# Attention queries rotated without their 1/rms, which scales the softmax exponential instead

## The chip, the core and the metric

The kernel runs on one core of one Trainium2 chip. The metric is the device time of one execution in microseconds (us); lower is better. A core has five engines with a queue of instructions each: TensorE (PE in the profile; its weight loads are listed as PEld), VectorE (DVE), ScalarE (ACT), GpSimd (POOL) and SyncE (SP), which issues most of the DMAs. They meet only at semaphores.

## What is computed

Two layers of a block with feed-forward, a mixer of windowed attention and gated linear attention, and a second feed-forward, for 256 tokens and 256 context tokens of width 1024. The change concerns the attention queries alone:

```python
q = axial_rope(rmsnorm(aq.reshape(B, S, ATTN_HEADS, ATTN_HEAD_DIM), q_norm_w), tabs)
k = axial_rope(rmsnorm(ak.reshape(B, S, ATTN_KV_HEADS, ATTN_HEAD_DIM), k_norm_w), tabs)
...
s_win = jnp.einsum('bnqhgd,bnkhd->bnhgqk', qb, kw).astype(jnp.float32) * scale
...
p = jax.nn.softmax(jnp.concatenate([s_win, s_ctx, s_sink], axis=-1), axis=-1).astype(v.dtype)
```

There are 8 query heads and 2 key heads of 128 dimensions. `rmsnorm` divides each query (one token of one head) by the root of its mean square and multiplies each dimension by a weight. `axial_rope` rotates pairs of dimensions by an angle of the token, for the 256 tokens of x only. In the first layer the context has queries too (512 in all), in the second only the 256 tokens of x.

## The kernel before

**Tiling.** Activations lie turned, with the feature on the 128 partitions and the tokens along the row: hH and hL hold the normed input as a high part in fp32r and the rest. Weights come in units of 1024 x 256 in `raw`; ScalarE casts each unit to WH (`prep`, line 683, two instructions), VectorE subtracts it to get WL (`prep`, line 1118, two), and TensorE makes three products for each pair of tiles (`unit_cols`, lines 1826, 1827 and 1832; `tile_cols`, lines 1846, 1847 and 1851), 24 for an output tile and 48 for a unit. Two unit buffers alternate. Sums land in PSUM, in the eight banks of PS.

**The stage that is changed** is `attn_proj`. Unit n is the values, n+1 the keys, n+2 to n+5 the queries (two heads each). In its loops j = 1 is the keys and j = 2 to 5 the query units; each has two tiles, one for a head, of 512 tokens (first layer; the keys in both) or 256. A tile goes through these steps, each on one engine:

- `squares` (ACT, line 814): PSUM to qsq.
- `qk_sums` (PE, line 2195): a plain fp32 product of qsq with a matrix of ones, which sums over the partitions and leaves the sum in every one of them, in bank 6 or 7.
- `rsq` (ACT, lines 821 and 824): logarithm and exponential, which gives 1/rms in qrs.
- `normed` (DVE, line 1425): PSUM times the weight times qrs, into qn.
- `swaps` (PE, line 2200): a plain fp32 product that exchanges the dimensions of each pair; it overwrites the PSUM bank of the unit.
- `cosines`, `sines`, `rotated` (DVE, lines 1433, 1438 and 1443): the two products and their sum.
- `split` (ACT, line 830) and `low` (DVE, line 1450): the high and the low part for the score products.

**What sets the order.** Every engine's order is written out by hand; nothing is scheduled. PE does a unit, then `swaps` of two units back and `qk_sums` of the unit before, and then the next unit. After n+5 come the first gate tile, `swaps(4)`, `qk_sums(5)`, the scores of the first set, the second gate tile with `swaps(5)` in its middle, and the third.

**Attention** follows, in sets of one key head and 128 queries: 8 in the first layer and 4 in the second. For a set PE makes `scores` (lines 1812 to 1814), DVE takes the maximum and forms the negative bias in two small steps (`maxima`, lines 1484 to 1492), ACT takes the exponential with the constant factor SCALE (`exps`, line 865), DVE divides (`scale`, line 1509), PE turns the probabilities in blocks (`turns`, line 2234; ACT and DVE split them, lines 876 and 1519) and multiplies them with the values. Gate tiles stand between. Line 2004 is used elsewhere: a product with `fold`, which adds the four quarters of 32 partitions. Line 1223 is a reduction of VectorE that first turns each block of 32 x 32. Line 1983 is a product with 32 columns of weights, four of which fill the four quarters of the output partitions.

Of the kernel before, what the change touches and what calls it, by code (L numbers as in the profile page):

```python
# [13 lines left out]
P = 128  # L14
D = 1024
LN_EXP = "natural_log_exp_and_others"
KT = D // P
# [86 lines left out]
def hybrid_backbone(nc, a, out):  # L104

    ctx = ExitStack()
    with ctx:
# [30 lines left out]
        epsc = sb("epsc", [P, 2])  # L138
# [5 lines left out]
        rstd = sb("rstd", [P, T2])  # L144

# [57 lines left out]
        cond_in = sem("cond_in")  # L203
# [4 lines left out]
        sink_in = sem("sink_in")  # L208
# [62 lines left out]
        qk_rot = sem("qk_rot")  # L271
        qk_hi = sem("qk_hi")
# [90 lines left out]
        def keys(qb):  # L363

            return (0, NTB) if qb < 2 else (S, 2)

# [110 lines left out]
        def _(sp):  # L477
# [50 lines left out]
            sp.dma_start(negsink[:], a["attn_sink"].rearrange("l h -> (l h)").partition_broadcast(P)).then_inc(sink_in, 16)  # L528
# [78 lines left out]
        def _(pool):  # L607
            nc.gpsimd.memset(epsc[:, 0:1], EPS)
            nc.gpsimd.memset(epsc[:, 1:2], 1.0).then_inc(eps_ready, 1)
# [50 lines left out]
        def _(act):  # L660
            act.dma_start(ident[:], a["c_ident"]).then_inc(ident_in, 16)
            act.dma_start(rows[0:16, 2, :], a["cond_rows"]).then_inc(cond_in, 16)
# [139 lines left out]
            def attn_proj(l):  # L802
                n = START[("attn_proj", l)]

                act.wait_ge(half_done, 2 * (n + 1))
                for b in (0, 2):
                    nc.scalar.copy(vH[:, b:b + 2, :], PS[:, 2 * b:2 * b + 2, 0:UW]).then_inc(v_hi, 1)

                def squares(j):
                    act.wait_ge(half_done, 2 * (n + j + 1))  # L810
                    for e, (t, T) in enumerate(qk_tiles(l, j)):
                        if t >= 2:
                            act.wait_ge(qk_ss, t - 1)
                        nc.scalar.activation(qsq[:, e, 0:T], PS[:, 2 * (j % 3) + e, 0:T], ACT.Square).then_inc(qk_sq, 1)

                def rsq(j):
                    for e, (t, T) in enumerate(qk_tiles(l, j)):
                        act.wait_ge(qk_ss, t + 1)
                        if t >= 2:
                            act.wait_ge(qk_n, t - 1)  # L820
                        nc.scalar.activation(qrs[:, e, 0:T], PS[:, 6 + e, 0:T], ACT.Ln, bias=epsc[:, 0:1], scale=1.0 / P).then_inc(qk_ln, 1)
                    for e, (t, T) in enumerate(qk_tiles(l, j)):
                        act.wait_ge(qk_ln, t + 1)
                        nc.scalar.activation(qrs[:, e, 0:T], qrs[:, e, 0:T], ACT.Exp, scale=-0.5).then_inc(qk_rs, 1)

                def split(j):
                    for e, (t, T) in enumerate(qk_tiles(l, j)):
                        act.wait_ge(qk_rot, t + 1)
                        dst = kH[:, e, 0:T] if j == 1 else actH[:, 2 * (j - 2) + e, 0:T]
                        nc.scalar.copy(dst, qn[:, e, 0:T]).then_inc(qk_hi, 1)  # L830

                for j in range(1, 6):
                    prep(n + j + 1)
                    squares(j)
                    if j > 1:
                        rsq(j - 1)
                    if j > 2:
                        split(j - 2)
                prep(n + 7)
                gate_copy(l, 0, 0)  # L840
                rsq(5)
                split(4)
                exps(l, 0)
                gate_copy(l, 1, 7)
                split(5)
                gate_copy(l, 2, 6)

# [263 lines left out]
        def _(dve):  # L1111
# [300 lines left out]
            def attn_proj(l):  # L1412
# [6 lines left out]
                def normed(j):  # L1419
                    for e, (t, T) in enumerate(qk_tiles(l, j)):  # L1420
                        dve.wait_ge(qk_rs, t + 1)
                        if t >= 2:
                            dve.wait_ge(qk_ready, t - 1)
                        w = vecT[:, K_NORM + l:K_NORM + l + 1] if j == 1 else vecT[:, Q_NORM + l:Q_NORM + l + 1]
                        nc.vector.scalar_tensor_tensor(qn[:, e, 0:T], PS[:, 2 * (j % 3) + e, 0:T], w, qrs[:, e, 0:T],
                                                       ALU.mult, ALU.mult).then_inc(qk_n, 1)

                def cosines(j):
                    for e, (t, T) in enumerate(qk_tiles(l, j)):
                        dve.wait_ge(qk_n, t + 1)  # L1430
                        if t >= 2:
                            dve.wait_ge(qk_rot, t - 1)
                        nc.vector.tensor_tensor(qt[:, e, 0, :], qn[:, e, 0:S], ropeC[:], ALU.mult)
# [6 lines left out]
                def rotated(j):  # L1440
                    for e, (t, T) in enumerate(qk_tiles(l, j)):
                        dve.wait_ge(qk_parts, t + 1)
                        nc.vector.tensor_tensor(qn[:, e, 0:S], qt[:, e, 0, :], qt[:, e, 1, :], ALU.add).then_inc(qk_rot, 1)

                def low(j):
                    for e, (t, T) in enumerate(qk_tiles(l, j)):
# [3 lines left out]
                        nc.vector.tensor_tensor(lo, qn[:, e, 0:T], hi.bitcast(F32), ALU.subtract).then_inc(qk_ready, 1)  # L1450

                for j in range(1, 6):
                    prep(n + j + 1)
                    if j > 2:
                        cosines(j - 2)
                        sines(j - 2)
                        rotated(j - 2)
                        low(j - 2)
                    if j > 1:
                        normed(j - 1)  # L1460
                cosines(4)
                sines(4)
                rotated(4)
                prep(n + 7, only=0)
                low(4)
                normed(5)
                maxima(l, 0)
                cosines(5)
                sines(5)
                scale(l, 0)  # L1470
                rotated(5)
                low(5)
                prep(n + 7, only=1)

            def maxima(l, i):

                A0, (kv, qb) = set0[l], SETS[l][i]
                k0, nkb = keys(qb)
                for e in range(2):
# [10 lines left out]
                    nc.vector.scalar_tensor_tensor(small[:, 8 + 2 * e:10 + 2 * e], small[:, two], -SCALE, ns, ALU.mult, ALU.min).then_inc(at_negmax, 1)  # L1490
                    dve.wait_ge(at_negmax, done + 1)
# [283 lines left out]
            for l in range(DEPTH):  # L1775
                if l:
                    norm(3 * l)
                if l == 0:
                    dve.wait_ge(sink_in, 16)
# [27 lines left out]
        def _(pe):  # L1807
# [210 lines left out]
            pe.wait_ge(ident_in, 16)  # L2018
            pe.wait_ge(cond_in, 16)
# [164 lines left out]
            def attn_proj(l):  # L2184
                n = START[("attn_proj", l)]
                if l == 0:
                    pe.wait_ge(const_in, 16 * 4)
                first_two(3 * l + 1, rows_high, rows_low, 2, 1)

                def qk_sums(j):  # L2190
                    for e, (t, T) in enumerate(qk_tiles(l, j)):
                        pe.wait_ge(qk_sq, t + 1)
                        if t >= 2:
                            pe.wait_ge(qk_ln, t - 1)
                        mm(PS[:, 6 + e, 0:T], ones[:], qsq[:, e, 0:T], start=True, stop=True).then_inc(qk_ss, 1)

                def swaps(j):
                    for e, (t, T) in enumerate(qk_tiles(l, j)):
                        pe.wait_ge(qk_n, t + 1)
                        mm(PS[:, 2 * (j % 3) + e, 0:S], swap[:], qn[:, e, 0:S], start=True, stop=True).then_inc(qk_swap, 1)  # L2200

                for j in range(2, 6):
                    if j == 2:
                        pe.wait_ge(v_ready, 2 * l + 2)
                    elif j > 3:
                        pe.wait_ge(qk_parts, tile0 * l + 2 * (j - 3))
                    unit_cols(n + j, 2 * (j % 3), hH, hL, qtokens(l))
                    if j > 2:
# [4 lines left out]
                swaps(4)  # L2213
                qk_sums(5)
                scores(l, 0)
                pe.wait_ge(qk_ln, tile0 * (l + 1))
                gate_cols(l, 1, 7, 0, KT // 2)
                swaps(5)
                gate_cols(l, 1, 7, KT // 2, KT)
# [334 lines left out]
```

## Time and profile before

| | us |
|---|---|
| median of 3 runs | 2237.07 |
| lowest and highest | 2236.84, 2237.15 |
| the profiled execution | 2237.79 |
| its span, first to last instruction | 2235.9 |
| TensorE busy | 2211.9 |
| VectorE busy | 1391.4 |
| ScalarE busy | 901.9 |

The granted TensorE clock is 1.0 of full speed in the run's record. The span is read as a chain: at each moment some engine does what the end depends on. A time in the tables is the length of an instruction as recorded; matmuls overlap in the pipeline, so the distance between two starts, not the length, is what one costs its engine.

### The profile page before, as it was taken

What the parts mean: (1) busy time and instruction counts of PE and PEld (TensorE: products, weight loads), DVE (VectorE), ACT (ScalarE), POOL (GpSimd) and SP (SyncE); (2) the same over time, 40 slices, a digit from 0 to 9 for tenths busy, and PEclk for the clock granted to TensorE, in tenths of its full rate; (3) what the DMA queues carried; (4) which work ended last, traced back from release to release, by engine and by line L of the source; (5) the groups of instructions that cost most, each with busy time, mean ns of one, the idle gap of its engine ahead of it and who ended that gap; (6) DMA issues with size and microseconds to landing.
All of it is one profiled execution on the core that took longest, in us unless ns stands there. A gap on an engine that the chain in (4) does not pass through costs nothing.

```text
span 2235.9 us, 29911 instructions
## 1 busy us (share of the span) xinstructions
PE 2211.9 (99%) x12353; PEld 1926.3 (86%) x12353; DVE 1391.4 (62%) x1919; ACT 901.9 (40%) x1352; POOL 194.5 (9%) x264
## 2 busy tenths in 40 slices
PE   8999999999999999999999999999999999999999
PEld 7888888878888888888888898888889899999997
DVE  6988822568566564586763267665236967676754
ACT  4223212456644453342322143222126666555442
POOL 0000000000333340000000000000000033330000
PEclk9999999999999999999999999999999999999999
DMA  9776523210322212346552236565323233336864
GB/s 318 218 230 187 180 97 101 87 50 29 95 76 64 88 58 94 113 138 197 157 168 94 95 113 199 179 187 169 113 95 96 60 114 114 114 116 195 245 180 160
DMA packets 300383, 300.84 MB, mean 135 GB/s; under 512 B 9648, under 2 KB 267288, under 8 KB 300248
## 3 DMA queue, kind: packets, MB, share of 16 engines
q1 hardware_dynamic: 299648, 298.69, 43.2%
q8 instruction: 98, 1.61, 0.3%
q14 instruction: 37, 0.30, 0.0%
q10 hardware_dynamic: 600, 0.25, 0.0%
HBM read 297.86 MB, written 1.05 MB: 134 GB/s over the span
## 4 chain that ended last, share of the span: by engine, by line
PE 90%; DVE 5%; POOL 2%; ACT 1%; issue 1%; DMA 1%; SPq 0%; DVEq 0%; ACTq 0%
PE PS L1826 14%; PE PS L1827 14%; PE PS L1832 14%; PE PS L1813 6%; PE PS L1814 6%; PE PS L1812 6%; PE PS L1846 4%; PE PS L1851 4%; PE PS L1847 4%; PE PS L2361 2%; PE PS L2420 1%; PE PS L2372 1%; DVE WL L1118 1%; PE PS L2097 1%; PE PS L2096 1%; PE PS L2095 1%
## 5 line engine op out<-in xcount | busy, mean ns | idle before, releaser
L1118 DVE TENSOR_TENSOR WL<-raw,WH 128x1024 fp32r<-128x1024 f32 x412 | 497.6, 1245 | 344.4 <-ACT WH L683 343.5
L683 ACT CAST WH<-raw 128x1024 fp32r<-128x1024 f32 x412 | 412.5, 1048 | 376.9 <-PE PS L1814 259.5
L1826 PE MATMUL PS<-hH,WH 128*128 128x512 f32 (+1 forms) x1536 | 542.2, 363 | 1.3 <-DVE sg L1383 0.9
L1827 PE MATMUL PS<-hL,WH 128*128 128x512 f32 (+1 forms) x1536 | 538.5, 361 | 0.0
L1832 PE MATMUL PS<-hH,WL 128*128 128x512 f32 (+1 forms) x1536 | 335.4, 361 | 0.0
L1826 PEld LDWEIGHTS PS<-hH,WH 128*128 128x128 f32 x1536 | 290.1, 189 | 46.4 <-issue 1.2
L1827 PEld LDWEIGHTS PS<-hL,WH 128*128 128x128 f32 x1536 | 290.5, 189 | 43.9 <-issue 1.2
L1832 PEld LDWEIGHTS PS<-hH,WL 128*128 128x128 f32 x1536 | 264.0, 189 | 44.1
L1146 DVE SCALAR_TENSOR_TENSOR mraw<-mraw,cst 128x1024 f32<-128x1024 f32 x196 | 242.5, 1280 | 18.3 <-DMA mraw<-in_w_mod 17.3
L1812 PE MATMUL PS<-hidH,WH 128*128 128x512 f32 (+1 forms) x576 | 214.6, 373 | 0.0
L1813 PE MATMUL PS<-hidL,WH 128*128 128x512 f32 (+1 forms) x576 | 214.1, 372 | 0.0
L1814 PE MATMUL PS<-hidH,WL 128*128 128x512 f32 (+1 forms) x576 | 214.1, 372 | 0.0
L791 ACT ACTIVATE sg<-PS 128x512 f32<-128x512 f32 (+1 forms) x44 | 24.0, 545 | 288.1 <-PE PS L1832 279.6
L1846 PE MATMUL PS<-hH,WH 128*128 128x512 f32 (+1 forms) x384 | 128.9, 348 | 0.0
L1812 PEld LDWEIGHTS PS<-hidH,WH 128*128 128x128 f32 x576 | 108.6, 188 | 19.0
L1813 PEld LDWEIGHTS PS<-hidL,WH 128*128 128x128 f32 x576 | 108.6, 188 | 18.9
L1814 PEld LDWEIGHTS PS<-hidH,WL 128*128 128x128 f32 x576 | 108.6, 188 | 18.5
L1847 PE MATMUL PS<-hL,WH 128*128 128x512 f32 (+1 forms) x384 | 124.4, 336 | 0.0
L785 ACT ACTIVATE sg<-PS 128x512 f32<-128x512 f32 (+1 forms) x44 | 24.0, 545 | 211.0 <-PE PS L1832 206.3
L1387 DVE TENSOR_TENSOR sg<-sg,PS 128x512 f32<-128x512 f32 (+1 forms) x44 | 27.3, 620 | 126.4 <-ACT sg L791 126.3
L1851 PE MATMUL PS<-hH,WL 128*128 128x512 f32 (+1 forms) x384 | 93.4, 337 | 0.0
L1641 DVE TENSOR_TENSOR dq<-dq,gkq 128x1024 f32<-128x1024 f32 (+1 forms) x56 | 62.1, 1110 | 47.3 <-ACT dq L986 46.9
(261 smaller groups left out, 3511.8 us busy)
## 6 DMA issues: line engine op xcount, KB each, us to landing
raw<-in_ffn_w SPq DMA_DIRECT2D x176, 512.0 KB, 5.2
mraw<-in_w_mod SPq DMA_DIRECT2D x132, 512.0 KB, 4.7
raw<-in_w_in SPq DMA_DIRECT2D x52, 1024.0 KB, 5.3
raw<-in_ffn_w SPq DMA_DIRECT2D x44, 1024.0 KB, 4.9
raw<-in_w_branch_attn SPq DMA_DIRECT2D x8, 1024.0 KB, 5.2
raw<-in_w_branch_gla SPq DMA_DIRECT2D x8, 1024.0 KB, 5.1
raw<-in_w_out SPq DMA_DIRECT2D x8, 1024.0 KB, 5.1
mfirst_b<-in_w_mod SPq DMA_DIRECT2D x8, 512.0 KB, 11.9
```

The lines of the kernel that those rows point to most:

```text
L683: nc.scalar.copy(half(WH, n % 2, e, rows), half(raw, n % 2, e, rows)).then_inc(hi_ready, 1)
L1118: nc.vector.tensor_tensor(half(WL, n % 2, e, rows), half(raw, n % 2, e, rows), half(WH, n % 2, e, rows).bitcast(F32), ALU.subtract).then_i ...
L1146: ins = nc.vector.scalar_tensor_tensor(mod_sums(c), mod_buf(p), by, mod_sums(c), ALU.mult, ALU.add)
L1812: mm(o, wh, ah, start=start, stop=False, skip_group_check=rest)
L1813: mm(o, wh, al, start=False, stop=False, skip_group_check=rest)
L1814: return mm(o, wl, ah, start=False, stop=stop, skip_group_check=rest)
L1826: mm(o, wh[:, kt, cols], rh[:, kt, 0:T], start=kt == 0, stop=False)
L1827: mm(o, wh[:, kt, cols], rl[:, kt, 0:T], start=False, stop=False)
L1832: ins = mm(o, wl[:, kt, cols], rh[:, kt, 0:T], start=False, stop=kt == KT - 1)
L1846: mm(o, wh[:, kt, cols], rh[:, kt, 0:T], start=kt == 0, stop=False)
L1847: mm(o, wh[:, kt, cols], rl[:, kt, 0:T], start=False, stop=False)
L1851: ins = mm(o, wl[:, kt, cols], rh[:, kt, 0:T], start=False, stop=kt == KT - 1)
```

## The change

**Queries are rotated without 1/rms.** The rotation is linear, so the factor can be applied later: a score of a query is the unscaled score times the query's 1/rms times SCALE. That factor differs by query, and in the scores a query is a partition, so it is a per-partition factor of the exponential. ScalarE copies the query tile out of PSUM times the weight (`weighted`), into qn or qrs by turns, and `rsq` and `normed` remain for the keys alone (`k_rsq`, `k_normed`).

**The squares are summed another way.** VectorE reduces the squares in turned blocks of 32 x 32 (`square_sums`, one instruction for both tiles), so that a token's four partial sums lie in four quarters of the partitions; TensorE adds the quarters with `fold`, for four heads at a time, in four products of 32 output partitions and 16 or 8 columns (`q_sums`). ScalarE takes the root of 16 or 8 columns (`q_rsq`) into rq. The matrix of ones is used for the keys alone.

**The bias** of the exponential needs one more small step on VectorE in `maxima`, since it must be multiplied by a factor of the query.

**Order and buffers.** `swaps(1)` stands between the two tiles of unit n+3, and `swaps(j)` behind unit n+j. Two buffers are new (640 bytes per partition together); all that is laid out behind them moves up by 640 bytes. Two semaphores are merged into others: `cond_in` into `ident_in` and `sink_in` into `const_in`.

New names:

```diff
+        qred = sb("qred", [P, HEADS * T2 // 32])
+        rq = sb("rq", [P, HEADS * NTB])
...
+        def rotated_buf(j):
+
+            return qn if j % 2 else qrs
+
+        def squares_buf(l, j):
+
+            return qsq[:].rearrange("p e t -> p (e t)")[:, 0:2 * (T2 if j == 1 else qtokens(l))]
```

ScalarE:

```diff
+                    if j == 2:
+                        act.wait_ge(qk_ss, 2 * (l + 1))
+                    elif j > 2:
+                        act.wait_ge(q_red, 4 * l + j - 2)
...
+                def weighted(j):
+                    act.wait_ge(half_done, 2 * (n + j + 1))
+                    if j == 2:
+                        act.wait_ge(qk_n, 2 * (l + 1))
+                    else:
+                        act.wait_ge(qk_ready, tile0 * l + 2 * (j - 2))
                     for e, (t, T) in enumerate(qk_tiles(l, j)):
...
+                        nc.scalar.activation(rotated_buf(j)[:, e, 0:T], PS[:, 2 * (j % 3) + e, 0:T], ACT.Copy,
+                                             scale=vecT[:, Q_NORM + l:Q_NORM + l + 1]).then_inc(q_n, 1)
+
+                def q_rsq(g):
+                    own = slice(g * GRP * qtokens(l) // P, (g + 1) * GRP * qtokens(l) // P)
+                    act.wait_ge(q_tot, 2 * l + g + 1)
+                    nc.scalar.activation(rq[:, own], PS[:, 6, own], ACT.Ln, bias=epsc[:, 2:3]).then_inc(q_ln, 1)
+                    act.wait_ge(q_ln, 2 * l + g + 1)
+                    nc.scalar.activation(rq[:, own], rq[:, own], ACT.Exp, scale=-0.5).then_inc(q_rs, 1)
...
-                for j in range(1, 6):
-                    prep(n + j + 1)
...
+                prep(n + 2)
+                squares(1)
+                prep(n + 3)
+                squares(2)
+                k_rsq()
+                weighted(2)
+                prep(n + 4)
+                split(1)
+                for j in range(3, 6):
+                    if j > 3:
+                        prep(n + j + 1)
+                    if j == 5:
+                        q_rsq(0)
+                    weighted(j)
                     squares(j)
...
+                    split(j - 1)
                 prep(n + 7)
                 gate_copy(l, 0, 0)
...
-                                             scale=SCALE, accum_out=small[:, 16 + g:17 + g])
+                                             scale=head_scales(l)[:, GRP * kv + g, qb:qb + 1], accum_out=small[:, 16 + g:17 + g])
```

VectorE:

```diff
+                def square_sums(j):
+                    dve.wait_ge(q_sq, 8 * l + 2 * (j - 1))
+                    own = slice((j - 2) * qtokens(l) // 16, (j - 1) * qtokens(l) // 16)
+                    nc.vector.tensor_reduce(qred[:, own], squares_buf(l, j).rearrange("p (b i) -> p b i", i=32), AX.X, ALU.add,
+                                            apply_transpose=True).then_inc(q_red, 1)
...
+                dve.wait_ge(q_rs, 2 * l + kv + 1)
...
-                    nc.vector.scalar_tensor_tensor(small[:, 8 + 2 * e:10 + 2 * e], small[:, two], -SCALE, ns, ALU.mult, ALU.min).then_inc(at_negmax, 1)
-                    dve.wait_ge(at_negmax, done + 1)
+                    by = head_scales(l)[:, GRP * kv + 2 * e:GRP * kv + 2 * e + 2, qb]
+                    nc.vector.scalar_tensor_tensor(small[:, 8 + 2 * e:10 + 2 * e], small[:, two], -1.0, by, ALU.mult, ALU.mult).then_inc(at_negmax, 1)
+                    dve.wait_ge(at_negmax, 2 * done + 1)
+                    nc.vector.tensor_tensor(small[:, 8 + 2 * e:10 + 2 * e], small[:, 8 + 2 * e:10 + 2 * e], ns, ALU.min).then_inc(at_negmax, 1)
+                    dve.wait_ge(at_negmax, 2 * done + 2)
```

TensorE:

```diff
+                def q_sums(g):
+                    pe.wait_ge(q_red, 4 * l + 2 * (g + 1))
+                    pe.wait_ge(qk_ln, 2 * (l + 1))
+                    w = GRP * qtokens(l) // P
+                    parts = qred[:, 4 * g * w:4 * (g + 1) * w].rearrange("p (x u) -> p u x", u=4)
+                    for u in range(4):
+                        lanes = slice(32 * u, 32 * u + 32)
+                        ins = mm(PS[lanes, 6, g * w:(g + 1) * w], fold[:, lanes], parts[:, u], start=True, stop=True)
+                    ins.then_inc(q_tot, 1)
...
-                for j in range(2, 6):
...
-                    unit_cols(n + j, 2 * (j % 3), hH, hL, qtokens(l))
-                    if j > 2:
-                        swaps(j - 2)
-                    qk_sums(j - 1)
...
+                pe.wait_ge(v_ready, 2 * l + 2)
+                unit_cols(n + 2, 4, hH, hL, qtokens(l))
+                k_sums()
+                unit_cols(n + 3, 0, hH, hL, qtokens(l), between=3 * [nothing] + [lambda: swaps(1)] + 3 * [nothing])
+                swaps(2)
+                pe.wait_ge(qk_parts, tile0 * l + 2)
+                unit_cols(n + 4, 2, hH, hL, qtokens(l))
+                swaps(3)
+                q_sums(0)
+                pe.wait_ge(qk_parts, tile0 * l + 4)
+                unit_cols(n + 5, 4, hH, hL, qtokens(l))
+                swaps(4)
                 pe.wait_ge(qk_parts, tile0 * l + 6)
                 gate_cols(l, 0, 0)
...
+                swaps(5)
+                q_sums(1)
                 scores(l, 0)
...
+                gate_cols(l, 1, 7)
+                pe.wait_ge(q_ln, 2 * (l + 1))
                 gate_cols(l, 2, 6)
```

**ScalarE in the first layer**, from the cast of unit n+2 on, before (qsq are squares, qrs<-PS the logarithm, qrs<-qrs the exponential, WH a cast):

```order
L683 CAST WH<-raw 128x8x128 x2
L814 ACTIVATE qsq<-PS 128x512 x2
L683 CAST WH<-raw 128x8x128 x2
L814 ACTIVATE qsq<-PS 128x512 x2
L821 ACTIVATE qrs<-PS,epsc 128x512 x2
L824 ACTIVATE qrs<-qrs 128x512 x2
L683 CAST WH<-raw 128x8x128 x2
L814 ACTIVATE qsq<-PS 128x512 x2
L821 ACTIVATE qrs<-PS,epsc 128x512 x2
L824 ACTIVATE qrs<-qrs 128x512 x2
```

and changed (line 853 is `weighted`, 867 `split`):

```order
L702 CAST WH<-raw 128x8x128 x2
L835 ACTIVATE qsq<-PS 128x512 x2
L702 CAST WH<-raw 128x8x128 x2
L835 ACTIVATE qsq<-PS 128x512 x2
L841 ACTIVATE qrs<-PS,epsc 128x512 x2
L844 ACTIVATE qrs<-qrs 128x512 x2
L853 ACTIVATE qrs<-PS,vecT 128x512 x2
L702 CAST WH<-raw 128x8x128 x2
L867 CAST kH<-qn 128x512 x2
L853 ACTIVATE qn<-PS,vecT 128x512 x2
L835 ACTIVATE qsq<-PS 128x512 x2
```

The logarithm and the exponential of a query tile are gone, a copy with the weight stands in their place, and the cast of unit n+4 stands behind the root and the weighted copy.

**TensorE in the first layer**, between unit n+4 and unit n+5, before:

```order
L1832 MATMUL PS<-hH,WL 128x512 x8
L2200 MATMUL PS<-qn,swap 128x256 x2
L2195 MATMUL PS<-qsq,ones 128x512 x2
L1826 MATMUL PS<-hH,WH 128x512
L1827 MATMUL PS<-hL,WH 128x512
```

and changed (line 2259 is `q_sums`):

```order
L1890 MATMUL PS<-hH,WL 128x512 x8
L2269 MATMUL PS<-qn,swap 128x256 x2
L2259 MATMUL PS<-qred,fold 32x16 x4
L1884 MATMUL PS<-hH,WH 128x512
L1885 MATMUL PS<-hL,WH 128x512
```

The two products of 512 columns with ones have become four of 16 columns, and only at every second unit.

**VectorE in the first set of attention**, one half of `maxima`, before:

```order
L1484 TENSOR_TENSOR PS<-PS,amask 128x2x128
L1486 TENSOR_REDUCE small<-PS 128x2
L1490 SCALAR_TENSOR_TENSOR small<-small,negsink 128x2
L1492 TENSOR_TENSOR small<-small,negsink 128x2
L1484 TENSOR_TENSOR PS<-PS,amask 128x2x128
L1486 TENSOR_REDUCE small<-PS 128x2
```

and changed:

```order
L1539 TENSOR_TENSOR PS<-PS,amask 128x2x128
L1541 TENSOR_REDUCE small<-PS 128x2
L1546 SCALAR_TENSOR_TENSOR small<-small,rq 128x2
L1548 TENSOR_TENSOR small<-small,negsink 128x2
L1550 TENSOR_TENSOR small<-small,negsink 128x2
L1539 TENSOR_TENSOR PS<-PS,amask 128x2x128
L1541 TENSOR_REDUCE small<-PS 128x2
```

One step of 128x2 is added between the maximum and the bias.

## Rows read from the trace of the kernel before

**Rows 1.** The page: busy time of each engine
```profile
PE 2211.9 (99%) x12353; PEld 1926.3 (86%) x12353; DVE 1391.4 (62%) x1919; ACT 901.9 (40%) x1352; POOL 194.5 (9%) x264
```

**Rows 2.** The line of the sums: duration ns min/median/max, first and last start, forms
```profile
L2195 PE MATMUL PS<-qsq,ones x40: 378/592/593, 432.6 to 1741.0; 128*128 128x512 f32 x24, 128*128 128x256 f32 x16
```

**Rows 3.** Timeline, TensorE, first layer: start us, length us, line, operation, idle before
```profile
432.64 1.88 PE L2195 MATMUL PS<-qsq,ones 128*128 128x512 f32 x4
...
434.59 0.40 PE L1827 MATMUL PS<-hL,WH 128*128 128x512 f32 x1
...
497.84 1.03 PE L2234 MATMUL PS<-ident,prob 128*128 128x128 f32 x8
```

**Rows 4.** Timeline, TensorE, second layer, the same stage
```profile
1719.27 1.03 PE L2195 MATMUL PS<-qsq,ones 128*128 128x256 f32 x4
1720.16 0.39 PE L1826 MATMUL PS<-hH,WH 128*128 128x256 f32 x1
...
1723.14 0.28 PE L1826 MATMUL PS<-hH,WH 128*128 128x256 f32 x1
...
1728.33 0.39 PE L1826 MATMUL PS<-hH,WH 128*128 128x256 f32 x1 [0.43 <-DVE qt L1438]
...
1739.38 1.13 PE L2200 MATMUL PS<-qn,swap 128*128 128x256 f32 x4 [0.43 <-DVE qn L1425]
...
1752.13 1.09 PE L2234 MATMUL PS<-ident,prob 128*128 128x128 f32 x8 [1.39 <-DVE prob L1509]
```

**Rows 5.** Timeline, TensorE, start of the program and one fold product
```profile
15.41 1.07 PE L1983 MATMUL PS<-mraw,cst 128*32 128x256 f32 x16
16.30 1.05 PE L1983 MATMUL PS<-mfirst_a,cst 128*32 128x256 f32 x16
...
85.95 0.33 PE L2004 MATMUL PS<-mrow,fold 128*128 128x64 f32 x2
...
86.40 0.40 PE L1827 MATMUL PS<-hL,WH 128*128 128x512 f32 x1
```

**Rows 6.** Line 1983, weight loads of 32 columns
```profile
L1983 PEld LDWEIGHTS PS<-mraw,cst x32: 105/110/111, 15.4 to 32.3; 128*32 128x32 f32 x32
```

**Rows 7.** Timeline, ScalarE, second layer: squares, logarithm, exponential of the keys
```profile
1712.86 0.38 ACT L814 ACTIVATE qsq<-PS 128x256 f32<-128x256 f32 x1 [0.42 <-PE PS L2195]
1713.14 1.26 ACT L821 ACTIVATE qrs<-PS,epsc 128x512 f32<-128x512 f32 x2
1714.28 1.16 ACT L824 ACTIVATE qrs<-qrs 128x512 f32<-128x512 f32 x2
```

**Rows 8.** Timeline, VectorE, second layer
```profile
1714.95 1.41 DVE L1425 SCALAR_TENSOR_TENSOR qn<-PS,vecT,qrs 128x512 f32<-128x512 f32 x2 [5.15 <-ACT qrs L824]
1716.40 2.36 DVE L1118 TENSOR_TENSOR WL<-raw,WH 128x1024 fp32r<-128x1024 f32 x2
```

**Rows 9.** Line 1223, the turned reduction: duration ns min/median/max
```profile
L1223 DVE TRANSPOSE_TENSOR_REDUCE mrow<-mraw x15: 1239/2305/2312, 78.6 to 1545.5; 128x64 f32<-128x2048 f32 x12, 128x32 f32<-128x1024 f32 x3
```

**Rows 10.** Timeline, VectorE: small steps after a maximum; last scaling of a set
```profile
547.88 0.62 DVE L1509 TENSOR_SCALAR prob<-prob,small 128x256 f32<-128x256 f32 x2
...
1784.21 0.16 DVE L1490 SCALAR_TENSOR_TENSOR small<-small,negsink 128x2 f32<-128x2 f32 x1
1784.40 0.16 DVE L1492 TENSOR_TENSOR small<-small,negsink 128x2 f32<-128x2 f32 x1
```

**Rows 11.** Timeline, TensorE: transposes of that set
```profile
548.67 1.03 PE L2234 MATMUL PS<-ident,prob 128*128 128x128 f32 x8
```

**Rows 12.** Waits of TensorE in the whole run: us in total, times, longest
```profile
PE PS L2234 <- DVE prob L1509: 4.8, 5, 1.4
...
PE PS L2234 <- DVE ptL L1519: 0.7, 2, 0.3
```

**Rows 13.** Groups by form: products that read unmoved and moved tiles
```profile
L1827 PE MATMUL PS<-hL,WH 128*128 128x512 f32 x1120 | 436.4, 390 | 0.0
...
L1813 PE MATMUL PS<-hidL,WH 128*128 128x512 f32 x480 | 186.9, 389 | 0.0
```

More of the change, by code:

```diff
@@ L271, in hybrid_backbone @@
         qk_rot = sem("qk_rot")
+        q_n = sem("q_n")
+        q_sq = sem("q_sq")
+        q_red = sem("q_red")
+        q_tot = sem("q_tot")
+        q_ln = sem("q_ln")
+        q_rs = sem("q_rs")
         qk_hi = sem("qk_hi")
@@ L661, in _ @@
             act.dma_start(ident[:], a["c_ident"]).then_inc(ident_in, 16)
[L662 removed]
+            act.dma_start(rows[0:16, 2, :], a["cond_rows"]).then_inc(ident_in, 16)
             act.dma_start(ones[:], a["c_ones"]).then_inc(ones_in, 16)
@@ L816, in rsq @@
-                def rsq(j):
-                    for e, (t, T) in enumerate(qk_tiles(l, j)):
[L818 to L824, printed above, removed]
+                        nc.scalar.activation(squares_buf(l, j)[:, e * T:(e + 1) * T], PS[:, 2 * (j % 3) + e, 0:T],
+                                             ACT.Square).then_inc(qk_sq if j == 1 else q_sq, 1)
@@ new lines, in k_rsq @@
+                def k_rsq():
+                    for e in range(2):
+                        act.wait_ge(qk_ss, 2 * l + e + 1)
+                        nc.scalar.activation(qrs[:, e, :], PS[:, 6 + e, :], ACT.Ln, bias=epsc[:, 0:1], scale=1.0 / P).then_inc(qk_ln, 1)
+                    for e in range(2):
+                        act.wait_ge(qk_ln, 2 * l + e + 1)
+                        nc.scalar.activation(qrs[:, e, :], qrs[:, e, :], ACT.Exp, scale=-0.5).then_inc(qk_rs, 1)
+                def weighted(j):
[4 more added lines that the diff above has]
+                        act.wait_ge(qk_ready, tile0 * l + 2 * (j - 2))
+                    for e, (t, T) in enumerate(qk_tiles(l, j)):
+                        nc.scalar.activation(rotated_buf(j)[:, e, 0:T], PS[:, 2 * (j % 3) + e, 0:T], ACT.Copy,
+                                             scale=vecT[:, Q_NORM + l:Q_NORM + l + 1]).then_inc(q_n, 1)
@@ L1417, in attn_proj, with k_normed @@
                                             ALU.subtract).then_inc(v_ready, 1)
[L1419 to L1425, printed above, removed]
+                def k_normed():
+                    for e in range(2):
+                        dve.wait_ge(qk_rs, 2 * l + e + 1)
+                        nc.vector.scalar_tensor_tensor(qn[:, e, :], PS[:, 2 + e, :], vecT[:, K_NORM + l:K_NORM + l + 1], qrs[:, e, :],
                                                        ALU.mult, ALU.mult).then_inc(qk_n, 1)
@@ L1449, in low @@
                         lo = kL[:, e, 0:T] if j == 1 else actL[:, 2 * (j - 2) + e, 0:T]
[L1450 to L1463, printed above, removed]
+                        nc.vector.tensor_tensor(lo, rotated_buf(j)[:, e, 0:T], hi.bitcast(F32), ALU.subtract).then_inc(qk_ready, 1)
+                prep(n + 2)
+                prep(n + 3)
+                k_normed()
+                cosines(1)
+                square_sums(2)
+                sines(1)
+                rotated(1)
+                prep(n + 4)
+                cosines(2)
+                low(1)
+                for j in range(3, 6):
+                    if j > 3:
+                        prep(n + j + 1)
+                    sines(j - 1)
+                    rotated(j - 1)
+                    cosines(j)
+                    square_sums(j)
+                    low(j - 1)
                 prep(n + 7, only=0)
-                low(4)
-                normed(5)
+                sines(5)
+                rotated(5)
                 maxima(l, 0)
-                cosines(5)
-                sines(5)
+                low(5)
                 scale(l, 0)
-                rotated(5)
-                low(5)
                 prep(n + 7, only=1)
@@ L2186, in attn_proj, with k_sums @@
                 if l == 0:
-                    pe.wait_ge(const_in, 16 * 4)
+                    pe.wait_ge(const_in, 16 * 5)
                 first_two(3 * l + 1, rows_high, rows_low, 2, 1)
[L2190 to L2195, printed above, removed]
+                def k_sums():
+                    for e in range(2):
+                        pe.wait_ge(qk_sq, 2 * l + e + 1)
+                        mm(PS[:, 6 + e, :], ones[:], qsq[:, e, :], start=True, stop=True).then_inc(qk_ss, 1)
@@ new lines, in swaps @@
+                        mm(PS[:, 2 * (j % 3) + e, 0:S], swap[:], rotated_buf(j)[:, e, 0:S], start=True, stop=True).then_inc(qk_swap, 1)
+                pe.wait_ge(v_ready, 2 * l + 2)
[5 more added lines that the diff above has]
+                unit_cols(n + 4, 2, hH, hL, qtokens(l))
```

54 lines of the change are left out of this document (21 added, 33 removed).

## The prediction

> **What bounds the kernel now.** The page's busy times come first: TensorE is busy for 2211.9 of 2235.9 us, VectorE for 62% and ScalarE for 40% [rows 1]. So the time is the length of TensorE's list of products plus its few gaps. An instruction taken from another engine is worth nothing by itself; one taken from TensorE is worth its slot, and a wait of TensorE is worth its length. The second view is the timeline of TensorE where the sums of squares stand, in either layer [rows 3, 4], which gives the slots. The third is TensorE's waits: over the whole run the transposes wait 5 times for the scaled probabilities, 4.8 us together, and twice for ptL, 0.7 us [rows 12]. In the second layer's attn_proj two gaps of 0.43 us come from the rotation chain, and 1.39 us are lost ahead of the first transposes [rows 4].
>
> **What is removed from TensorE.** The sums are 40 recorded products, two for a tile, 24 of 512 columns and 16 of 256 [rows 2]. The keys keep 8 of the 24, so 16 of each kind go. In the first layer a pair of tiles starts at 432.64, and the second product behind it at 434.59; less one slot of 0.23 (which is what 512 columns in fp32r cost), the pair took 1.72 us [rows 3]. Four pairs go: 6.9 us. In the second layer the sums run from 1719.27 to 1720.16, 0.89 us for four products of 256 columns [rows 4]; half of 1.72 is 0.86, and the rest is the change back to the next weights, which stays, because the swaps that stand beside the sums stay. Four pairs: 3.4 us. Together **10.3 us**.
>
> **What is added to TensorE.** Four `q_sums` of four products, two passes each: 32 recorded products of 32 output partitions and 16 or 8 columns. The trace has none so narrow. The nearest of that shape (128 rows, 32 weight columns) ran 16 in 0.89 us, 15.41 to 16.30, or 0.056 us each, although with 256 columns [rows 5]. From above, one full product with `fold` (two passes, 128 weight columns) runs from 85.95 to 86.40 less a slot of 0.23, so 0.22 us [rows 5]; four of these are 0.88 for a `q_sums`. From below the bound is 0. I take the row of the same shape, 8 x 0.056 = 0.45 for each, **1.8 us** in all; the range is 0 to 3.5.
>
> A rule speaks against this. The narrow products all use the full 128 rows, and their weight loads were recorded at 110 ns each [rows 6], twice the 0.056 us at which the pairs followed each other, so there they overlapped. The Trainium skill (TensorE: Matmul & The Clock Gate, Part 3: Packing small matmuls) says that a weight load overlaps with running matmuls only when the row group differs, which it does not here. By that rule a pair would cost its load and its product, and the rows disagree with it for the products at 15.41; with 256 columns a load can hide, and whether it can with 16 is open. That is the second rival below.
>
> **What moves in attn_proj, second layer** (the tight one: a unit takes 5.8 us, not 10.9). `swaps(1)` now stands after half of unit n+3, and there its chain is short of time. `squares(2)` now starts when both key sums are done, at 1712.86, where one of its tiles had been done before, so the logarithm begins 0.28 later than 1713.14 and the exponential 0.28 later than 1714.28 [rows 7]; `k_normed` moves from 1714.95 to 1715.23 and its second tile ends near 1716.64 (1.41 long) [rows 8]. TensorE ends the key sums at about 1712.66 and half a unit is 2.9 us (1720.16 to 1723.14 with the change back) [rows 4], so it arrives at 1715.5, waits 0.5 for the first tile and 0.2 for the second: 0.7 us new. From there on a round of TensorE is 5.8 + 1.0 (swaps), in two of them + 0.45. VectorE's round is a preparation 2.3, four steps of 0.7 and the turned sum, between half of 1.24 and 1.24 [rows 8, 9]: 5.7 to 6.3. ScalarE's is 3.9. Both fit, so the two old gaps of 0.43 go: each unit's sine product now comes right after its swap, with a unit of other products before the next use of the bank. The scores of the first set then start about 1.6 us earlier than before, VectorE no longer has `normed` and two cosine products between the scores and the probabilities, and I get the last scaling done at 1748.6 with TensorE there at 1747.9: a wait of 0.65 in place of 1.39. Together the waits go from 2.25 to 1.35: **0.9 us gained**. In the first layer half a unit is 5.4 us, swaps(1) finds its keys ready by about 1 us, nothing waited in that stage and nothing will; TensorE reaches the first transposes, 497.84 before [rows 3], 6.0 us earlier, and the probabilities are there 4 us before it.
>
> **What the added step in `maxima` costs.** A dependent step of two columns comes 0.19 to 0.20 us after the one before it (1784.21 to 1784.40) [rows 10]. Each half of a set has one more, so the last probabilities of each of the 12 sets are 0.4 us later. Where TensorE has slack that is free, where it waited already it is paid in full. It waits for probabilities 5 times [rows 12]; the one at 1752.13 is dealt with above, the other four pay 0.4 each, 1.6. One of the two waits for ptL, in the second layer, stands behind a ScalarE queue that is itself late, 0.4 more. In the first layer a set's last scaling (547.88, 0.62 long) ends 0.2 before its transposes start at 548.67 [rows 10, 11]: 0.3 more, and 0.1 for the set ahead of it. Sum **2.4 us lost**; the bounds are 0 (the steps hide behind the exponentials) and 24 x 0.2 = 4.8.
> A figure of the Trainium skill (VectorE: DVE Perf Modes, the TRN2 errata) is 58 cycles at 0.96 GHz plus the columns for a step that reads SBUF, an estimate of 0.06 us; by it the sum would be 0.8 and not 2.4. The row shows three times that between dependent steps, and I go by the row.
>
> **The rest costs nothing.** The exponential's factor read per partition instead of a constant: it reads a bias that way already. The wait for q_rs ahead of `maxima`: rq of the first four heads is ready one round before, those of the others during the first set. The merged semaphores wait for transfers that are long done or were waited for anyway. The shift of 640 bytes: see the last rival.
>
> **The sum.** 10.3 - 1.8 + 0.9 - 2.4 = 7.0 us. The profiled execution had a span of 2235.9 and took 2237.79; it would be 2228.9 and 2230.8. The median was 0.7 below the profiled one, so the forecast for the median is 2237.07 - 7.0 = **2230.1**.
>
> **The rivals.**
> 1. *Small prices at their ends.* If the narrow products cost as little as half a slot and the added steps hide (1.0 and 0.5), the gain is 10.3 - 1.0 + 0.9 - 0.5 = 9.7, 2227.4. For it: VectorE's busy share of 62% [rows 1]. Against it: four of the waits are ends of just this chain.
> 2. *The weight loads do not overlap.* Each pass costs its load of 0.11 [rows 6] and some 0.03 for the columns: 32 x 0.14 = 4.5 instead of 1.8, gain 4.3, 2232.8. For it: with 8 or 16 columns there is no long product to hide a load behind. Against it: the overlap at 15.41 [rows 5]. (This is what the Trainium skill's rule gives.)
> 3. *The attention loop pays every step.* All 24 steps on the path, 4.8 instead of 2.4: gain 4.6, 2232.5. For it: a set later by 0.4 shifts everything behind it on VectorE and ScalarE. Against it: the 2-block sets at the end of the first layer leave TensorE's gates between.
> 4. *Slower.* All tiles behind rstd move by 640 bytes, among them hidden activations, attention activations and merged rows, the moving side of about 2,700 products. If the new start address costs each of them over 7.0/2700 = 2.6 ns of its slot of 227, the gain is gone; at 5 ns the time is 2237.07 - 7.0 + 13.5 = 2243.6. Against it: products that read hidL and those that read hL, which lie elsewhere, take 389 and 390 ns on average [rows 13], and the new addresses keep every power of two up to 128 bytes. For it: nothing in the trace, and no row with such a shift.
>
> **How the numbers follow.** The forecast 0.50 (its own range 2228.8 to 2231.6), rival 1 0.20, rival 2 0.10, rival 3 0.12, rival 4 0.04, and 0.04 for something of another kind on either side. The range that leaves out two in ten runs from 2227.0 to 2233.2. A measurement tells 0.2%, 4.5 us, from no change, which puts the border at 2232.6. Rival 1 and the forecast lie well below it, rival 3 on it, rival 2 just above. So faster 0.80, within 0.2% 0.15, slower 0.05.
>
> **What would show it.** In the changed profile the line of the ones has 4 recorded products of 512 columns in each layer and no others; 32 narrow ones stand after swaps(3) and swaps(5), and the distance from the start of four of them to the next product tells rival 2 (0.45 or 1.1). TensorE's waits should list swaps(1) in the second layer with 0.5 to 0.7, no wait for the sines there, about 0.6 at the first transposes, and 1.6 or so more in all at the others; many new short waits would mean rival 3. The products on hidL must still average 389 ns; a few ns more is rival 4. I am wrong if attn_proj of the first layer gains clearly less than 6 us, for there nothing but TensorE's list is at work.

## The result: 2241.6 us, slower by 0.19%

| | before | changed |
|---|---|---|
| median, us (17 runs each) | 2237.56 | 2241.6 |
| lowest and highest | 2236.72, 2238.07 | 2241.33, 2242.33 |
| ratio, 95% interval | | 1.0019 (1.0012 to 1.0025) |
| span of the profiled execution | 2235.9 | 2239.8 |

The forecast was 2230.1 with a range to 2233.2. The page of the changed kernel, busy time of each engine, answers to [rows 1]:

```profile
PE 2216.8 (99%) x12353; PEld 1919.9 (86%) x12353; DVE 1394.9 (62%) x1935; ACT 901.1 (40%) x1344; POOL 194.8 (9%) x265
```

TensorE is busy 4.9 us longer than before, though the sums for the queries are gone. Its timeline in the two stages where work was taken out answers to [rows 3, 4]. The first and third line are the key sums of a layer, the second and last the first transposes of its attention, and between them in the second layer stands `swaps(1)`:

```profile
434.58 1.88 PE L2250 MATMUL PS<-qsq,ones 128*128 128x512 f32 x4
...
493.39 1.04 PE L2304 MATMUL PS<-ident,prob 128*128 128x128 f32 x8
...
1717.24 1.88 PE L2250 MATMUL PS<-qsq,ones 128*128 128x512 f32 x4
...
1722.39 1.36 PE L2269 MATMUL PS<-qn,swap 128*128 128x256 f32 x4 [0.41 <-DVE qn L1467]
...
1754.25 1.09 PE L2304 MATMUL PS<-ident,prob 128*128 128x128 f32 x8 [0.58 <-DVE prob L1567]
```

From the key sums to the first transposes it takes 493.39 - 434.58 = 58.8 us in the first layer, where it took 497.84 - 432.64 = 65.2, and 37.0 us in the second, where it took 41.2 (the key sums there began at 1710.94). So the stage that was changed is 6.4 and 4.2 us shorter. The time came back elsewhere:

| stage of TensorE, us | before | changed | difference |
|---|---|---|---|
| start to the key sums of layer 1 | 432.6 | 434.6 | +1.9 |
| key sums to first transposes, layer 1 | 65.2 | 58.8 | -6.4 |
| from there to the key sums of layer 2 | 1213.1 | 1223.9 | +10.8 |
| key sums to first transposes, layer 2 | 41.2 | 37.0 | -4.2 |
| from there to the end | 483.8 | 485.6 | +1.8 |

The code of the third stage is that of before but for the small step in `maxima` and the factor of the exponential. The groups by form show where it went; a column is the mean length in ns of one recorded product. Products of 512 columns on hL, on hidL and hidH, and on actL:

```profile
L1885 PE MATMUL PS<-hL,WH 128*128 128x512 f32 x1120 | 436.2, 389 | 0.0
...
L1872 PE MATMUL PS<-hidH,WL 128*128 128x512 f32 x480 | 189.6, 395 | 0.0
...
L1871 PE MATMUL PS<-hidL,WH 128*128 128x512 f32 x480 | 189.6, 395 | 0.0
...
L1905 PE MATMUL PS<-actL,WH 128*128 128x512 f32 x128 | 50.4, 394 | 0.0
...
L2154 PE MATMUL PS<-WH,hidL 128*128 128x512 f32 x88 | 34.7, 394 | 0.0
```

Products on hL take 389 ns, where they took 390. Those on hidL take 395 where they took 389 [rows 13], and there are 480 x 3 of them, 2.7 us more for each 480. The recorded length is not what a product costs, but the distance between starts grew with it: from 227 to 233 ns from one product on hidL to the next, in the median of the 480. All tiles with the longer products lie behind the two new buffers, 640 bytes higher than before.

### The profile page after: what moved, and what is told of

Its sections match the earlier page's. It is cut to its first block, busy times and chain, and to the rows that moved or that the text cites. A ratio compares the mean times of both kernels' runs of the same rounds, so it can differ in the third digit from the quotient of the medians.

```text
span 2239.8 us, 29904 instructions
## 1 busy us (share of the span) xinstructions
PE 2216.8 (99%) x12353; PEld 1919.9 (86%) x12353; DVE 1394.9 (62%) x1935; ACT 901.1 (40%) x1344; POOL 194.8 (9%) x265
## 4 chain that ended last, share of the span: by engine, by line
PE 89%; DVE 6%; POOL 2%; ACT 1%; issue 1%; DMA 1%; SPq 0%; DVEq 0%; ACTq 0%
PE PS L1884 14%; PE PS L1885 14%; PE PS L1890 14%; PE PS L1870 6%; PE PS L1872 6%; PE PS L1871 6%; PE PS L1909 4%; PE PS L1904 4%; PE PS L1905 4%; PE PS L2431 2%; PE PS L2490 1%; DVE WL L1163 1%; PE PS L2442 1%; PE PS L2154 1%; PE PS L2152 1%; PE PS L2153 1%
```

## Experiments

A is the theory that the start of the moved tiles costs TensorE its time, B that the changed attention does. The positions below are starts within a partition, modulo 256 bytes. In the built kernel xT starts at byte 1152, and the others follow from the sizes of the tiles in the order in which they are declared. Before, hH, hL, WH, WL, hidH, hidL, actH and actL all start 128 past a multiple of 256. In the changed kernel hidH, hidL, actH and actL start at a multiple; epsc, which also grew, from 8 to 16 bytes, moved nothing.

**The shift alone, and its size.** The first adds to the kernel before:

```diff
         rstd = sb("rstd", [P, T2])
+        pad = sb("pad", [P, 160])
```

> The kernel before with 640 unused bytes per partition behind rstd and nothing else: the tiles behind it start at 0 instead of 128 bytes past a multiple of 256, as in the changed kernel. Theory A (the start address of the moved tiles costs TensorE): products on hidH and hidL take 395 ns instead of 389, and the time is 2237 + 11 = 2248 us. Theory B (the shift is innocent, the changed attention costs the time): 2237 us, 389 ns.

Measured 2249.8 us against 2237.2 of before in the same session, ratio 1.0056 (1.0041 to 1.0071). Groups by form of that kernel, answering to [rows 13]:

```profile
L1828 PE MATMUL PS<-hL,WH 128*128 128x512 f32 x1120 | 436.1, 389 | 0.0
...
L1814 PE MATMUL PS<-hidL,WH 128*128 128x512 f32 x480 | 189.6, 395 | 0.0
```

Nothing but the place of the tiles was changed, and the products on hidL went from 389 to 395 ns and the time up by 12.6 us. B's claim that the shift is innocent falls. Then the changed kernel with the shift made up to 768 bytes, three times 256:

```diff
         rq = sb("rq", [P, HEADS * NTB])
+        pad = sb("pad", [P, 32])
```

> The changed kernel with 128 more unused bytes behind rq, so that the shift is 768 bytes, three times 256. Theory A: the products on hidH are back at 389 ns and the time is 2241.6 - 11.5 = 2230 us, about the forecast. Theory B: it stays at 2241 us.

Measured 2229.6 us, ratio 0.9966 (0.9953 to 0.9979): 7.6 us faster than before and 12 faster than the changed kernel, by 128 unused bytes. Products on hidL and their like are back:

```profile
L1872 PE MATMUL PS<-hidL,WH 128*128 128x512 f32 x480 | 186.7, 389 | 0.0
```

Two more shifts of the kernel before, by `[P, 32]` and by `[P, 64]` in the same place:

> The kernel before with 128 unused bytes. If what counts is the start modulo 256, this is as slow as the shift of 640: 2248 us, 395 ns. If it is the size of the shift or a larger modulus, it is not: 2237 us.

Measured 2249.9 us, 1.0056 (1.0041 to 1.0071): as slow as the shift of 640.

> The kernel before with 256 unused bytes. If what counts is the start modulo 256: unchanged, 2237 us, 389 ns. If any shift costs, 2248 us.

Measured 2237.2 us, 1.0001 (0.9991 to 1.0010): nothing. So the position modulo 256 counts and the size of the shift does not.

**The place itself, or the place against the weights?** A product reads two tiles. In the next kernel the pad stands ahead of xT, so that all tiles move by 128 together:

> The kernel before with 128 unused bytes ahead of the first tile, so that every tile, weights and normed input too, starts at a multiple of 256. If the start of the moving side itself is what costs, the 1120 x 3 products of 512 columns on hH and hL get slower as well, by 5.6 ns each, and the time is 2237 + 12.6 + 19 or more = 2269 us or more. If what costs is how the moving tile lies against the weights it is multiplied with, all pairs lie as before: 2237 us, 389 ns everywhere.

Measured 2236.2 us, 0.9994 (0.9983 to 1.0006), 389 ns for the products on hidL. All the tiles named above start at a multiple of 256 now. For hidL that was slow in the third kernel, and here it is not slow: what counts is not hidL's own start. With a second pad of 128 bytes behind rstd:

> 128 bytes ahead of the first tile and 128 behind rstd: weights and hH at a multiple of 256, hidden and attention activations 128 past one. If the start of the moving side itself costs: hid products at 389 ns, hH products at 395. If the two sides' positions to each other cost: hid products at 395 ns, hH products at 389, 2250 us.

Measured 2249.8 us, 1.0054 (1.0032 to 1.0077): hidL starts 128 past a multiple, as in the kernel before, and is slow again with 395 ns; the weights stand at a multiple now. And the other way round, with the pad between hL and raw, so that hH and hL stay and the weights go with all the rest:

```diff
         hL = sb("hL", [P, KT, T2], F32R)
+        pad_mid = sb("pad_mid", [P, 32])
         raw = sb("raw", [P, 2, UN])
```

> The kernel before with 128 unused bytes between hL and raw: the weights and all behind them move by 128, hH and hL do not. If the position of the two sides to each other counts, the hid products stay at 389 ns and the products of 512 columns on hH and hL, 3 x 1312, go to 395: 22 us slower, 2259. If the start of the moving tile itself counts, hid products go to 395 and hH stays: 2250.

Measured 2254.2 us, 1.0075 (1.0056 to 1.0093). Groups by form, hL of 512 and of 256 columns and hidL of 512:

```profile
L1828 PE MATMUL PS<-hL,WH 128*128 128x512 f32 x1120 | 442.1, 395 | 0.0
...
L1814 PE MATMUL PS<-hidL,WH 128*128 128x512 f32 x480 | 186.8, 389 | 0.0
...
L1828 PE MATMUL PS<-hL,WH 128*128 128x256 f32 x416 | 101.1, 281 | 0.0
```

Now hL takes 395 ns, though it did not move, and hidL 389, though it did. So the start of neither tile by itself counts, but that of one against the other. The time rose by 17 us where I expected 22. The last line shows a reason: products of 256 columns take 281 ns at this offset and took 283 before, the other way round, and some 3,600 of them that read hH or hL and are 1 to 2 ns shorter make 4 to 7 us. Both the slow and the fast side are effects of 1 to 6 ns on products of 283 and 389.

In every one of these kernels raw and the small tiles stand or move together with the weights, so another tile than WH and WL could be the partner that counts. A product that reads no weights tells. ptL and vH both lie behind the pad and move against raw, WH and everything else ahead of it, but not against each other; the kernel before first, that with the shift of 640 behind it:

```profile
L1813 PE MATMUL PS<-ptL,vH 128*128 128x512 f32 x40 | 15.7, 392 | 0.0
```

```profile
L1814 PE MATMUL PS<-ptL,vH 128*128 128x512 f32 x40 | 15.7, 392 | 0.0
```

They stay at 392 ns. Only products with one tile on either side of the pad changed, so it is the two tiles that a product reads. At this offset it does not matter which of the two is the weights: in `PS<-WH,hidL` (394 ns in the changed kernel, 389 before) hidL is the weights and WH the moving tile.

**Other offsets.** By `[P, 16]` and `[P, 8]` behind rstd:

> The kernel before with 64 unused bytes behind rstd. If any start other than that of the weights modulo 256 costs, hid products take 395 ns or so (2250 us); if only an offset of 128 does, 389 (2237 us). No theory gives a number in between.

> The same with 32 unused bytes: 389 ns and 2237 us if only the offset of 128 costs, more if every offset does.

Measured 2242.6 us (1.0022, 1.0011 to 1.0034) for 64 bytes and 2250.7 us (1.0057, 1.0032 to 1.0077) for 32. At 64 bytes the products differ among themselves, which no theory had said:

```profile
L1813 PE MATMUL PS<-hidH,WH 128*128 128x512 f32 x480 | 189.1, 394 | 0.0
L1815 PE MATMUL PS<-hidH,WL 128*128 128x512 f32 x480 | 188.2, 392 | 0.0
L1814 PE MATMUL PS<-hidL,WH 128*128 128x512 f32 x480 | 186.3, 388 | 0.0
...
L2096 PE MATMUL PS<-WH,hidH 128*128 128x512 f32 x88 | 34.8, 396 | 0.0
```

At 32 bytes all of these take 395 or 396 ns. An offset that is no multiple of 256 cost time in each of the three cases that were tried (128, which 640 equals, 64 and 32); how much depends on the offset and on the product.

**The prices inside the forecast.** The padded kernel is the base for two kernels and the kernel before for one. The narrow sums issued twice:

```diff
-                    for u in range(4):
+                    for u in (0, 1, 2, 3, 0, 1, 2, 3):
```

> The changed kernel with the 128 bytes of padding, and every narrow sum of quarters issued twice (the second overwrites the first with the same values): 32 more recorded narrow products. If they cost what the forecast took, 0.056 us each, it is 1.8 us slower than the padded kernel, 2231.4; if each pays its weight load, 4.5 us, 2234.1; if they follow each other as in the padded kernel's trace, at about 0.025 us, 0.8 us, 2230.4.

Measured 2230.25 us against 2229.62 of the padded kernel, each known to about 1 us, so the times alone only exclude the 4.5. The timelines of TensorE in the first layer tell more. The padded kernel without and with a `q_sums` behind its swaps, and the doubled one:

```profile
445.59 1.03 PE L2270 MATMUL PS<-qrs,swap 128*128 128x256 f32 x4
...
446.69 0.40 PE L1886 MATMUL PS<-hL,WH 128*128 128x512 f32 x1
...
457.39 1.03 PE L2270 MATMUL PS<-qn,swap 128*128 128x256 f32 x4
458.35 0.26 PE L2260 MATMUL PS<-qred,fold 128*32 128x16 f32 x8
458.54 0.50 PE L1885 MATMUL PS<-hH,WH 128*128 128x512 f32 x1
458.88 0.39 PE L1886 MATMUL PS<-hL,WH 128*128 128x512 f32 x1
```

```profile
457.19 1.03 PE L2270 MATMUL PS<-qn,swap 128*128 128x256 f32 x4
458.15 0.33 PE L2260 MATMUL PS<-qred,fold 128*32 128x16 f32 x16
458.40 0.50 PE L1885 MATMUL PS<-hH,WH 128*128 128x512 f32 x1
458.75 0.40 PE L1886 MATMUL PS<-hL,WH 128*128 128x512 f32 x1
```

From the swaps to the first product on hL it takes 1.10 us with nothing between, 1.49 with 8 narrow products and 1.56 with 16. So one `q_sums` costs 0.39 us, and 8 narrow products more cost 0.07: most of the price does not depend on how many there are. The weight loads of the padded kernel show where it is paid:

```profile
458.35 0.16 PEld L2260 LDWEIGHTS PS<-qred,fold 128*32 128x32 f32 x8 [0.33 <-issue]
```

The loads stand idle for 0.33 us ahead of the first one, and then all 8, recorded at 106 to 110 ns each, start and end within 0.16. What fills the 0.33 us the trace does not show. A price of 0.11 or 0.14 for each product, with weight loads that do not overlap, is out.

The added step alone, in the kernel before:

```diff
+                    dve.wait_ge(at_negmax, 2 * done + 1)
+                    nc.vector.tensor_tensor(small[:, 8 + 2 * e:10 + 2 * e], small[:, 8 + 2 * e:10 + 2 * e], ns, ALU.min).then_inc(at_negmax, 1)
+                    dve.wait_ge(at_negmax, 2 * done + 2)
```

> The kernel before with the one added dependent step of two columns in each half of maxima (a minimum that changes nothing) and nothing else. Forecast: 2.0 to 2.4 us slower, 2239.5; if it hides, 2237.2; if every step is on the path, 4.8 us, 2242.0.

Measured 2240.9 us against 2237.5, ratio 1.0015 (1.0006 to 1.0024): 3.4 us, with an interval from 1.3 to 5.4. TensorE's waits of that kernel answer to [rows 12]:

```profile
PE PS L2236 <- DVE prob L1511: 6.1, 5, 1.8
...
PE PS L2236 <- DVE ptL L1521: 1.2, 2, 0.7
```

The transposes wait 7.3 us in all where they waited 5.5: the step is on the path. The 1.8 us of these two lines lie below the 2.4 of the forecast and the measured time above it; the interval does not decide between 2.4 and 4.8, it excludes 0.

`swaps(1)` behind the whole unit:

```diff
-                unit_cols(n + 3, 0, hH, hL, qtokens(l), between=3 * [nothing] + [lambda: swaps(1)] + 3 * [nothing])
+                unit_cols(n + 3, 0, hH, hL, qtokens(l))
+                swaps(1)
```

> The padded changed kernel with swaps(1) behind the whole unit n+3 instead of between its tiles. If the new wait of the second layer there (0.4 us, and 0.2 for the second tile) is the only effect of that place, it is 0.5 us faster, 2229.1; if the late swap holds up the unit behind it, which must wait for its sine product, it is 0.5 us slower or more.

Measured 2230.6 us, 0.9969 (0.9957 to 0.9980), which is not told from the padded kernel's 2229.6. Its waits of TensorE:

```profile
PE PS L1871 <- ACT mraw L900: 1.2, 1, 1.2
...
PE PS L2260 <- DVE qred L1484: 0.3, 1, 0.3
PE PS L1885 <- ACT WH L703: 0.2, 1, 0.2
```

The wait of 0.4 us at `swaps(1)` is gone, and 1.2, 0.3 and 0.2 us stand further down, because the key's rotation now ends later and with it the whole chain of the queries: the scores of the first set wait for a gate copy (line 900) behind it. From the key sums to the first transposes the second layer takes 38.2 us there (1742.70 - 1704.46) and 37.0 in the padded kernel (1742.60 - 1705.57), so within this stage the early swap is worth its wait by 1.2 us; the medians, 1.0 apart, do not tell it by themselves.

## Why the prediction was wrong

**The step that failed is "The rest costs nothing", the shift of 640 bytes.** It is rival 4, with a chance of 0.04. Two things in its case were mistaken. I took [rows 13] as evidence: 389 and 390 ns for tiles that lie elsewhere. But these tiles lie alike against the weights, all 128 bytes past a multiple of 256, so the rows could not have shown a difference; they held the one quantity constant that matters. And I wrote that the new addresses keep every power of two up to 128 bytes. That is true, and 640 is two and a half times 256; the kernels with shifts of 128 and 256 show that 256 is the one it had to keep. The rival's arithmetic was right in kind: about 5.6 ns on the products of 512 columns, some 2,200 of which read one moved tile (three lines of 480, three of 88, three of 128 and 144 more), is 12 us, and the shift alone measured 12.6.

**The rest of the sum held in total, not in each term.** With the shift made up to 768 bytes the kernel measured 2229.6 us; the forecast was 2230.1. The interval of its ratio is a gain of 4.7 to 10.5 us. By its steps, from the padded kernel's trace:

| step | forecast, us | measured, us |
|---|---|---|
| key sums to first transposes, layer 1 | -6.0 | -6.4 |
| the same, layer 2, waits included | -3.4 | -4.2 |
| from there to the key sums of layer 2 | +1.2 | +1.7 |
| layer 2, from the first transposes to the end | +1.2 | +0.8 |
| start to the first key sums | 0 | -0.6 |
| whole, profiled spans (medians) | -7.0 | -8.7 (-7.6) |

- *Removed sums*: 10.3 us as forecast. In the first layer a pair takes 2.81 - 1.10 = 1.71 us (445.29 to 448.10 with swaps and sums before, 445.59 to 446.69 with swaps alone now), in the second 0.86 where nothing waits. The line of the ones keeps 8 recorded products, 4 in each layer.
- *Narrow sums*: 0.39 us for each, 0.38 in the second layer, 1.5 in all where 1.8 was forecast. That the figure is close is luck: 8 x 0.056 stood for eight products that each cost something, and the runs show a step of about 0.3 us ahead of them and under 0.01 for each further one. Rival 2, that the weight loads do not overlap, is out. The Trainium skill's rule (TensorE: Matmul & The Clock Gate, Part 3) that a weight load overlaps running matmuls only in another row group is not borne out here: these loads are recorded at 106 to 110 ns and all use the full 128 rows, and 8 of them, with a product behind each, lie within 0.16 us.
- *A wait that the prediction did not see*: it says that nothing waited in the first layer's attn_proj. In the kernel before, the fourth swaps did:

```profile
480.38 0.30 PEld L2200 LDWEIGHTS PS<-qn,swap 128*128 128x128 f32 x2 [0.35 <-DVE qn L1425]
481.03 0.30 PEld L2200 LDWEIGHTS PS<-qn,swap 128*128 128x128 f32 x2 [0.36 <-DVE qn L1425]
```

They start 0.09 us late and take 1.19 us up to the sums at 481.57, where the others take 0.87: 0.4 us that stand only in the list of its weight loads and not in that of its products. These waits are gone with the queries' `normed`, and they make up the 0.4 by which the first layer gained more than forecast.
- *Waits in the second layer*: `swaps(1)` waits 0.41 us for its first tile and, by its length of 1.36 in place of 1.02, 0.3 more (forecast 0.5 and 0.2); the first transposes wait 0.58 (forecast 0.65, before 1.39); the two gaps of 0.43 are gone. By the starts those gaps had cost 0.69 and 0.60 us (1726.88 to 1728.55 where 0.98 is usual, 1737.82 to 1739.38 where it is 0.96), which makes up about half of the 0.8 by which this stage beat its forecast.
- *The added step*: paid where TensorE waited. In the second layer the transposes of the third and fourth set now wait 1.31 and 0.76 us, where they waited 1.26 and 0.36:

```profile
1780.00 1.09 PE L2304 MATMUL PS<-ident,prob 128*128 128x128 f32 x8 [1.31 <-DVE prob L1567]
...
1791.12 1.09 PE L2304 MATMUL PS<-ident,prob 128*128 128x128 f32 x8 [0.76 <-DVE prob L1567]
```

The fourth pays its 0.4, the third only 0.05. In the first layer it is the same: 1.32 us became 1.33, 0.52 became 0.92, and a wait of 0.22 is new. So two of the four waits that the forecast charged in full pay next to nothing, and in the padded kernel the waits for probabilities behind the first transposes rose by 1.1 us, not 1.6. Rival 3, that all 24 steps are paid, does not fit that. The two stages together are 2.5 us longer, near the forecast of 2.4, but what makes up the rest of that is not shown; the step by itself costs between 1.3 and 5.4 us.
- *Merged semaphores*: the first product waits 7.0 us for its rows where it waited 6.1, but the feed-forward begins no later for it, and the stage to the first key sums is 0.6 shorter in the padded kernel.

## What to carry to other kernels

A new buffer moves every buffer that is declared behind it, so check a change of the layout by itself: 128 unused bytes were worth 12 us here, more than the idea of the change. Where TensorE is the bound, keep the moving tiles and the weights of its frequent products at the same position modulo 256 bytes, and read the mean length of one product of untouched code in the trace after a change; 389 against 395 ns is the whole answer here. And when a wait is to be priced, take the distance between starts on both sides of it: the list of TensorE's waits left out 0.4 us here, and a gap of 0.43 in it was 0.6 to 0.7. When rows are to show that something costs nothing, ask first whether they differ in it.

## What the runs showed of the hardware

- The length of an fp32r product depends on where its two tiles, the moving one and the weights, lie against each other in the partition: for 512 columns 389 ns where the two starts agree modulo 256 bytes; on hidH and hidL 394 to 396 at an offset of 128 or 32, and 388 to 396 at 64 depending on the product. The distance from start to start goes from 227 to 233 ns with it. A common shift of both changes nothing.
- For 256 columns the sign is the opposite: 281 or 282 against 283 ns at an offset of 128, and 278 to 280 on actL and hidL at 32 and 64. The kernel has many of these in its second layer, so a layout with another offset there might gain a few us; that was not tried. Why the offset matters stays open: the traces show lengths, not the reads behind them.
- Eight products of 32 output columns and 16 moving columns, in four quarters, cost 0.39 us between plain fp32 products and the next fp32r ones, and eight more only 0.07, although each weight load is recorded at 106 to 110 ns. The first load comes after 0.33 us of idle.
